# The first two experts do their down product behind their own up product, the third and later ones one expert later

## Chip, cores and metric

One core of one Trainium2 chip. The time is that of the whole kernel on the device, in microseconds; each shown time is a run of its own, and the profile is one further execution.

## What is computed

Two residual layers of a decoder for 512 tokens of width 1024. Each layer has a mixer and then a mixture of experts; the change touches the experts alone, which run once in each layer. Cut to what matters:

```python
def expert_block(args):
    xb, e = args
    return (jax.nn.silu(xb @ w1[e]) * (xb @ w3[e])) @ w2[e]
...
expert_idx = g_sel[:, None].astype(jnp.int32) * EXPERTS_PER_GROUP + top_i.astype(jnp.int32)
return routed_experts(xf, expert_idx, gates, w1, w3, w2).reshape(b, t, d)
```

There are 32 experts (numbered from 0 here), each with w1 and w3 of 1024 x 512 and w2 of 512 x 1024, in float32. Every token goes to two of them, weighted by its gates.

## The kernel before, in words

The program is written engine by engine: each engine has its own list of instructions for a stage, and semaphores join them. The router stage writes every token's normed row to `sorted_rows` in memory, behind its expert's rows. The stage `experts` then goes over the 32 experts with up to 48 rows each (`MB`):

- TensorE, `turn_rows` (L669): the expert's rows are transposed into bank `ps_x`. VectorE, `gain_rows` (L738): they are copied to `xT` with the norm's gain. There are two tiles `xT`.
- TensorE, `up_expert` (L681, L682): 8 steps with w1 and w3, 32 matmuls. ScalarE, `silu` (L799); VectorE, `hidden` (L746): the product with the second half, into `hid`. The next up product waits for it (`hid_done`, L675), as it does for `xT_out`.
- TensorE, `turn_hidden` (L703): `hid` is transposed; ScalarE, `copy_hidden` (L794), brings it to `hidT`.
- TensorE, `down_expert` (L711): 16 matmuls with w2. VectorE, `split_low` (L754, L758), and ScalarE, `split_high` (L806), cut the result into a high and a low part.
- VectorE, `select` (L771, L773): a 0/1 matrix that takes the expert's rows to tokens. TensorE, `spread` (L733): 8 matmuls with that matrix, four behind an up product and four in the middle of a down product. VectorE, `add` (L783): eight additions into `x`, weighted by the gates.

"Up n", "down n", "hidden n" and so on below are these steps for expert n.

Two orders exist. From expert `OWN` = 19 on, the down product of expert n stands behind its own up product (own order), with the spread of expert n - 1 around it. Below 19, down n stands behind up n + 1, and its spread one expert later still:

```python
for n in range(1, OWN):
    up_expert(pe, n, n - 2)
    turn_hidden(pe, n - 1)
    turn_rows(pe, slot(n + 1), use(n + 1))
    down_expert(pe, n - 1, n - 2)
```

The weights are 96 pieces of 2048 KB, numbered 3n, 3n + 1 (w1, w3 of expert n) and 3n + 2 (w2). They go round through 11 units of SBUF (`place`), so piece 11 + j may be loaded once piece j was used: once up was done for a w1 or w3, once down was done for a w2 (`freed`, L847). SyncE issues them in the order of their numbers (L583; in halves at L590 for the up weights of the last two experts), each expert's rows ahead of its pieces (L824), and waits where a piece is not free. Pieces 0 to 9 are loaded in the router stage, piece 10 at the start of `experts`; piece 11 needs up 0, 12 up 0, 13 down 0, 14 and 15 up 1, 16 down 1, 17 and 18 up 2, 19 down 2. The row load in front of pieces 12, 15 and 18 needs the turned rows of experts 1, 2 and 3.

Of the kernel before, what the change touches and what calls it, by code (L numbers as in the profile page):

```python
# [37 lines left out]
N_EXP = 32  # L38
# [582 lines left out]
def experts(nc, c, ctx, ps, x, xrows, r, gain_dram, wts, ahead):  # L621
# [33 lines left out]
    slots_made, far_out = c.sem("slots_made"), c.sem("further_slot_out")  # L655
    diag_made, row_done, row_out, own = c.sem("diag_made"), c.sem("row_done"), c.sem("row_out"), c.sem("dve_own")

    LAST, OWN = N_EXP - 1, 19
    XSLOT, XUSES = N_EXP % SLOTS, N_EXP // SLOTS
    slot = lambda n: n % SLOTS  # L660
    use = lambda n: n // SLOTS
# [3 lines left out]
    def turn_rows(pe, j, u):  # L665
        pe.wait_ge(rows_in[j], 16 * u + 16)
        nc.tensor.ldweights(c.half[:, :], tile_position=(0, 0))
        for i in range(XG):
            last = nc.tensor.transpose(ps_x[:, i:XG * P:XG], x_rows[j][:, i, :], c.ident[:, :])  # L669
        last.then_inc(xT_done, 1)  # L670
# [15 lines left out]
    def up_expert(pe, n, before):  # L686
        def first_half():
            for part in range(2):
                wts.arrived(pe, n, part)

        def second_half():
            if n in HALVED:
                for part in range(2):
                    pe.wait_ge(wts.rest_landed[HALVED.index(n)][part], 16)

        up(pe, n, n % 2, wts.view(n, 0), wts.view(n, 1), first_half, second_half)
        spread(pe, before, range(TT // 2))
# [91 lines left out]
    def gate_of(n):  # L789
        return lambda t: r.gate[:, t, n:n + 1]  # L790
# [35 lines left out]
    with nc.Block() as block:  # L826
# [56 lines left out]
        @block.tensor  # L883
        def _(pe):
            keep_warm(nc, c, ps_y[0], 40)
            for j in range(2):
                pe.wait_ge(diag_made, j + 1)
                nc.tensor.matmul(ps_c[j][:, :], c.ones[:, :], (cut, acts)[j][:, :],
                                 start=True, stop=True).then_inc(row_done, 1)
            pe.wait_ge(gain_in, 16)  # L890
            turn_rows(pe, 0, 0)
            up_expert(pe, 0, -1)
            turn_rows(pe, 1, 0)
            for n in range(1, OWN):
                up_expert(pe, n, n - 2)
                turn_hidden(pe, n - 1)
                turn_rows(pe, slot(n + 1), use(n + 1))
                down_expert(pe, n - 1, n - 2)
            turn_hidden(pe, OWN - 1)
            spread(pe, OWN - 2, range(TT // 2))  # L900
            down_expert(pe, OWN - 1, OWN - 2)
            for n in range(OWN, N_EXP):
                up_expert(pe, n, n - 1)
                if n < LAST:
                    turn_rows(pe, slot(n + 1), use(n + 1))
                turn_hidden(pe, n)
                down_expert(pe, n, n - 1)
            spread(pe, LAST, range(TT))

            def more(e, b, m):  # L910
                n, u = m + N_EXP, m + XUSES

                def landed(part):
                    pe.wait_ge(wts.landed[EXTRA[part]], 16 * m + 16 * (LOADS[EXTRA[part]] + 1))

                def extra(part):
                    return wts.unit[EXTRA[part]][:, :].rearrange("p (k n) -> p k n", k=PARTS[part])

                def first_half():
                    landed(0)  # L920
                    landed(1)

                turn_rows(pe, XSLOT, u)
                up(pe, n, 0, extra(0), extra(1), first_half, lambda: None)
                turn_hidden(pe, n)
                landed(2)
                down(pe, n, extra(2), lambda i: None)
                spread(pe, n, range(TT))

            further(pe, more)  # L930

        @block.vector
        def _(dve):
            V = nc.vector
            link = chain(dve, own)
            dve.sem_inc(low_out, 1)
            for j, tile in enumerate((cut, acts)):
                V.tensor_tensor(tile[:, :].rearrange("p (t n) -> p t n", t=TT),
                                c.ident[:, :].rearrange("p (o n) -> p o n", o=1).to_broadcast([P, TT, P]),
                                r.row[:, :, j:j + 1].to_broadcast([P, TT, P]), ALU.mult).then_inc(diag_made, 1)  # L940
            for h in range(2):
                link(V.tensor_scalar(y[:, h, :].rearrange("p (t n) -> p t n", t=TT),
                                     c.ident[:, :].rearrange("p (o n) -> p o n", o=1).to_broadcast([P, TT, P]),
                                     0.0, None, ALU.mult))
            dve.wait_ge(slots_made, 8)
            dve.wait_ge(gain_in, 16)
            gain_rows(dve, 0, 0)
            for j in range(2):
                dve.wait_ge(row_done, j + 1)
                V.tensor_copy(row_of[:, j, :], ps_c[j][:, :]).then_inc(row_out, 1)  # L950
            dve.wait_ge(row_out, 2)
            dve.sem_inc(row_out, 1)
            gain_rows(dve, 1, 1)
            hidden(dve, 0, None)
            early, late = range(TT), range(TT, GROUPS)
            for n in range(1, OWN):
                if n >= 2:
                    split_low(dve, n - 2)
                    add(dve, n - 2, early, gate_of(n - 2))
                hidden(dve, n, n)  # L960
                gain_rows(dve, n + 1, (n + 1) % 2)
                select(dve, n - 1, slot_rows(n - 1))
                if n >= 2:
                    add(dve, n - 2, late, gate_of(n - 2))
            for n in range(OWN - 2, LAST):
                if n >= 0:
                    split_low(dve, n)
                select(dve, n + 1, slot_rows(n + 1))
                if n >= OWN - 1:
                    hidden(dve, n + 1, n + 1)  # L970
                    if n + 2 <= LAST:
                        gain_rows(dve, n + 2, n % 2)
                if n >= 0:
                    add(dve, n, range(GROUPS), gate_of(n))
            split_low(dve, LAST)
            add(dve, LAST, range(GROUPS), gate_of(LAST))

            def more(e, b, m):
                n = m + N_EXP
                gain_rows(dve, n, 0)  # L980
                V.tensor_copy(far_gate[:, :], r.gate[:, :, bass.ds(e, 1)].rearrange("p t o -> p (t o)")).then_inc(far_out, 1)
                V.tensor_tensor(far[:, 0:1], r.count[:, bass.ds(e, 1)], c.block_rows[:, bass.ds(b - 1, 1)],
                                ALU.subtract).then_inc(far_out, 1)
                dve.wait_ge(far_out, 6 * m + 2)
                V.tensor_scalar(far[:, 1:2], slot0[:, :], far[:, 0:1], float(MB), ALU.add, ALU.is_ge).then_inc(far_out, 1)
                V.tensor_tensor(far[:, 2:3], slot_row[:, bass.ds(e, 1)], far[:, 0:1], ALU.add).then_inc(far_out, 1)
                dve.wait_ge(far_out, 6 * m + 4)
                V.scalar_tensor_tensor(out=far[:, 2:3], in0=far[:, 2:3], scalar=-NO_ROW, in1=far[:, 1:2],
                                       op0=ALU.add, op1=ALU.mult).then_inc(far_out, 1)
                dve.wait_ge(far_out, 6 * m + 5)  # L990
                V.tensor_scalar(far[:, 3:4], far[:, 2:3], NO_ROW, None, ALU.add).then_inc(far_out, 1)
                dve.wait_ge(far_out, 6 * m + 6)
                hidden(dve, n, None)
                select(dve, n, far[:, 3:4])
                split_low(dve, n)
                add(dve, n, range(GROUPS), lambda t: far_gate[:, t:t + 1])
                dve.wait_ge(added, GROUPS * n + GROUPS)

            further(dve, more)

        @block.scalar
        def _(act):
            act.wait_ge(row_done, 2)
            silu(act, 0)
            for n in range(1, OWN):
                if n >= 2:
                    split_high(act, n - 2)
                silu(act, n)
                copy_hidden(act, n - 1)
            copy_hidden(act, OWN - 1)  # L1010
            if OWN >= 2:
                split_high(act, OWN - 2)
            for n in range(OWN, N_EXP):
                split_high(act, n - 1)
                silu(act, n)
                copy_hidden(act, n)
            split_high(act, LAST)

            def more(e, b, m):

                n = m + N_EXP
                silu(act, n)
                copy_hidden(act, n)
                split_high(act, n)

            further(act, more)
# [1718 lines left out]
```

## Time and profile before

| | us |
|---|---|
| median of 3 runs | 1823.58 (1823.37 to 1824.29) |
| the profiled execution | 1821.84 |
| its span, first to last instruction | 1820.1 |
| TensorE matmul busy | 1656.2 (91%) |
| VectorE busy | 1167.3 (64%) |
| ScalarE busy | 489.8 (27%) |
| mean granted TensorE clock | 0.966 |

The profile gives times from the span's start. The first expert stage begins its DMA issues at 516.5 us and its last down product ends at 985 us; the second one's begin at 1326 us. "PE" is TensorE, "DVE" VectorE, "ACT" ScalarE, "SPq" SyncE's queue. A timeline row is: start, duration, engine, line and operation, output and inputs, shapes, count, and in brackets the idle time before it with what ended it. DMA instructions issued by SyncE stand at their issue, not at their landing. A granted clock of 1.00 is 2.4 GHz, 0.50 is 1.2 GHz.

### The profile page before, as it was taken

The page shows a single profiled execution, that of the slowest core. Times are in us where ns is not written, and L with a number is a line of the kernel's source. Part 1 is how long each engine was busy: PE and PEld are TensorE (multiplying, and loading weights), DVE is VectorE, ACT ScalarE, POOL GpSimd, SP SyncE. Part 2 cuts the span into 40 slices and gives each one's busy share as a digit, 9 for nine tenths or more (in the row PEclk, how much of TensorE's full clock was granted, in tenths as well). Part 3 has the DMA queues.
Part 4 walks back from the last instruction along what each step waited for, and adds up shares of the span by engine and source line. Part 5 has one row for each costly group of instructions (what it writes and reads, how often), then busy time and mean ns, then how long its engine had stood idle before and what let it go on. Part 6 is the DMA issues. An engine that isn't in the chain of part 4 may idle for free. (4 is left out here: it accounts for less than half of the span.)

```text
span 1820.1 us, 27622 instructions
## 1 busy us (share of the span) xinstructions
PE 1656.2 (91%) x10944; PEld 888.5 (49%) x11073; DVE 1167.3 (64%) x1926; ACT 489.8 (27%) x854; POOL 181.1 (10%) x234
## 2 busy tenths in 40 slices
PE   6999989989969999999997999889779999999995
PEld 4666677855533333333332779654433333333332
DVE  5467877783337677777777533693427776777766
ACT  5253334453301111111112411573211111111112
POOL 2000734411100000000000000351100000000000
PEclk9999999999979999999998999999989999999997
DMA  5541000024769999999995220206669999999993
GB/s 159 154 134 35 6 3 4 3 94 165 292 262 406 425 425 424 426 424 424 425 424 222 88 93 24 93 2 258 272 244 426 425 424 425 425 426 424 424 421 132
DMA packets 101474, 471.46 MB, mean 259 GB/s; under 512 B 29152, under 2 KB 68064, under 8 KB 75744
## 3 DMA queue, kind: packets, MB, share of 16 engines
q1 hardware_dynamic: 99040, 461.26, 63.1%
q0 software_dynamic: 2304, 8.39, 1.1%
q8 instruction: 90, 1.47, 0.3%
q14 instruction: 40, 0.33, 0.0%
HBM read 452.85 MB, written 16.78 MB: 258 GB/s over the span
## 5 line engine op out<-in xcount | busy, mean ns | idle before, releaser
L681 PE MATMUL ps<-w_unit,xT 128*48 128x512 f32 x1024 | 451.7, 594 | 6.1 <-issue 4.6
L682 PE MATMUL ps<-w_unit,xT 128*48 128x512 f32 x1024 | 451.7, 594 | 0.0
L783 DVE SCALAR_TENSOR_TENSOR x<-ps,gate_by_expert,x 128x512 f32<-128x512 f32 x512 | 348.4, 744 | 137.3 <-PE ps L733 137.2
L681 PEld LDWEIGHTS ps<-w_unit,xT 128*48 128x48 f32 x1024 | 125.9, 123 | 311.0 <-issue 309.0
L711 PE MATMUL ps<-w_unit,hidT 128*48 128x512 f32 x1024 | 248.4, 605 | 12.1 <-issue 12.1
L806 ACT ACTIVATE y_high_low<-y_cut 48x512 fp32r<-48x512 f32 x128 | 80.4, 628 | 402.2 <-DVE y_cut L754 399.7
L733 PE MATMUL ps<-y_high_low,slots_to_tokens 128*128 128x512 f32 x512 | 158.1, 430 | 14.4 <-DVE y_high_low L758 13.2
L733 PEld LDWEIGHTS ps<-y_high_low,slots_to_tokens 128*128 128x128 f32 x512 | 88.0, 192 | 131.9 <-issue 66.1
L1245 PE MATMUL ps<-hT_high,w_high 128*128 128x512 f32 (+1 forms) x344 | 139.7, 406 | 10.0 <-PE ps L1247 3.7
L1247 PE MATMUL ps<-hT_high,w_low 128*128 128x512 f32 (+1 forms) x344 | 135.9, 395 | 0.0
L1246 PE MATMUL ps<-hT_low,w_high 128*128 128x512 f32 (+1 forms) x344 | 135.5, 394 | 0.0
L682 PEld LDWEIGHTS ps<-w_unit,xT 128*48 128x48 f32 x1024 | 125.9, 123 | 0.0
L711 PEld LDWEIGHTS ps<-w_unit,hidT 128*48 128x48 f32 x1024 | 60.3, 123 | 120.8 <-issue 120.8
L746 DVE TENSOR_TENSOR gate_act_hid<-gate_act_hid,ps 48x512 f32<-48x512 f32 x64 | 44.3, 692 | 111.0 <-ACT gate_act_hid L799 92.4
L353 PE MATMUL ps<-w_unit,yT 128*128 128x512 f32 x256 | 113.7, 596 | 1.7 <-PEq L78 1.7
L799 ACT ACTIVATE gate_act_hid<-ps 48x512 f32<-48x512 f32 x64 | 37.9, 592 | 274.1 <-PE ps L682 274.1
L754 DVE TENSOR_SCALAR y_cut<-ps 48x512 int32<-48x512 int32 x128 | 87.5, 684 | 5.5 <-PE ps L711 3.6
L758 DVE TENSOR_TENSOR y_high_low<-ps,y_cut 48x512 fp32r<-48x512 f32 x128 | 88.2, 689 | 4.0
L1443 POOL TENSOR_SCALAR_AFFINE_SELECT keep<-keep 128x256 f32<-128x256 f32 x32 | 20.4, 638 | 666.3 <-ACT keep L1420 666.2
L1245 PEld LDWEIGHTS ps<-hT_high,w_high 128*128 128x128 f32 (+1 forms) x344 | 64.3, 187 | 42.5 <-issue 27.1
L353 PEld LDWEIGHTS ps<-w_unit,yT 128*128 128x128 f32 x256 | 47.3, 190 | 54.6 <-issue 54.6
L1247 PEld LDWEIGHTS ps<-hT_high,w_low 128*128 128x128 f32 (+1 forms) x344 | 64.2, 187 | 15.9
(368 smaller groups left out, 2232.6 us busy)
## 6 DMA issues: line engine op xcount, KB each, us to landing
w_unit<-in_moe_w SPq DMA_DIRECT2D x184, 2048.0 KB, 27.4
w_unit<-in_moe_w SPq DMA_DIRECT2D x16, 1024.0 KB, 33.4
x_rows<-sorted_rows SPq DMA_DIRECT2D x64, 192.0 KB, 26.9
w_unit<-in_od_w_qkv SPq DMA_DIRECT2D x12, 1024.0 KB, 5.3
w_raw<-in_ev_w_in SPq DMA_DIRECT2D x10, 1024.0 KB, 6.9
sorted_rows<-bias SPq DMA_DIRECT2D x32, 192.0 KB, 5.6
w_unit<-in_ev_w_out SPq DMA_DIRECT2D x2, 2048.0 KB, 11.6
w_unit<-in_od_w_out SPq DMA_DIRECT2D x2, 2048.0 KB, 11.6
```

The source lines that it names most:

```text
L353: last = nc.tensor.matmul(ps_out[2 * (i % 2) + h][:, :], yT[:, f, tok(i)], w[h][:, f, :], start=f == 0, stop=f == KD - 1)
L681: nc.tensor.matmul(ps_1[0:MB, :], xT[b][:, k, :], w1[:, k, :], start=k == 0, stop=k == KD - 1)
L682: last = nc.tensor.matmul(ps_3[UP:UP + MB, :], xT[b][:, k, :], w3[:, k, :], start=k == 0, stop=k == KD - 1)
L711: last = nc.tensor.matmul(ps_y[h][half[h], :], hidT[:, k, :], w2[:, k, h * FF:(h + 1) * FF], start=k == 0, stop=k == KF - 1)
L733: nc.tensor.matmul(ps_c[t % 2 * 2 + h][:, :], sel_of(n)[:, t * P:(t + 1) * P], y[:, h, :], start=True, stop=True).then_inc(spread_out, 1)
L754: nc.vector.tensor_scalar(cut[half[h], :].bitcast(I32), ps_y[h][half[h], :].bitcast(I32), HIGH_BITS, None, ALU.bitwise_and).then_inc(maske ...
L758: nc.vector.tensor_tensor(y[half[1 - h], h, :], ps_y[h][half[h], :], cut[half[h], :], ALU.subtract).then_inc(low_out, 1)
L783: nc.vector.scalar_tensor_tensor(out=xs, in0=ps_c[i % 4][:, :], scalar=gate(t), in1=xs, op0=ALU.mult, op1=ALU.add).then_inc(added, 1)
L806: nc.scalar.activation(y[half[h], h, :], cut[half[h], :], ACT.Copy).then_inc(high_out, 1)
L1245: nc.tensor.matmul(out, lhsT[0], rhs[0], start=start, stop=False)
L1246: nc.tensor.matmul(out, lhsT[0], rhs[1], start=False, stop=False)
L1247: return nc.tensor.matmul(out, lhsT[1], rhs[0], start=False, stop=stop)
```

## The change

A number `EARLY` = 2 is added. Experts 0 and 1 go in own order, expert 2's up stands by itself, and from expert 3 to 18 the order is the old one. VectorE's and ScalarE's lists follow.

```diff
-    LAST, OWN = N_EXP - 1, 19
+    LAST, OWN, EARLY = N_EXP - 1, 19, 2
...
             turn_rows(pe, 0, 0)
-            up_expert(pe, 0, -1)
-            turn_rows(pe, 1, 0)
-            for n in range(1, OWN):
+            for n in range(EARLY):
+                up_expert(pe, n, n - 1)
+                turn_rows(pe, slot(n + 1), use(n + 1))
+                turn_hidden(pe, n)
+                down_expert(pe, n, n - 1)
+            up_expert(pe, EARLY, -1)
+            turn_rows(pe, slot(EARLY + 1), use(EARLY + 1))
+            for n in range(EARLY + 1, OWN):
                 up_expert(pe, n, n - 2)
                 turn_hidden(pe, n - 1)
                 turn_rows(pe, slot(n + 1), use(n + 1))
...
             hidden(dve, 0, None)
+            select(dve, 0, slot_rows(0))
+            for n in range(EARLY - 1):
+                split_low(dve, n)
+                select(dve, n + 1, slot_rows(n + 1))
+                hidden(dve, n + 1, n + 1)
+                gain_rows(dve, n + 2, n % 2)
+                add(dve, n, range(GROUPS), gate_of(n))
+            hidden(dve, EARLY, EARLY)
+            gain_rows(dve, EARLY + 1, (EARLY + 1) % 2)
             early, late = range(TT), range(TT, GROUPS)
-            for n in range(1, OWN):
-                if n >= 2:
-                    split_low(dve, n - 2)
-                    add(dve, n - 2, early, gate_of(n - 2))
+            for n in range(EARLY + 1, OWN):
+                split_low(dve, n - 2)
+                add(dve, n - 2, early, gate_of(n - 2))
                 hidden(dve, n, n)
                 gain_rows(dve, n + 1, (n + 1) % 2)
                 select(dve, n - 1, slot_rows(n - 1))
-                if n >= 2:
-                    add(dve, n - 2, late, gate_of(n - 2))
+                add(dve, n - 2, late, gate_of(n - 2))
...
             silu(act, 0)
-            for n in range(1, OWN):
-                if n >= 2:
-                    split_high(act, n - 2)
+            copy_hidden(act, 0)
+            for n in range(1, EARLY):
+                split_high(act, n - 1)
+                silu(act, n)
+                copy_hidden(act, n)
+            silu(act, EARLY)
+            for n in range(EARLY + 1, OWN):
+                split_high(act, n - 2)
                 silu(act, n)
                 copy_hidden(act, n - 1)
```

TensorE, first stage, behind up 0 (+ is the change, - is before; `x_rows_332` are expert 1's rows, units 273 and 274 its w1 and w3, unit 272 is expert 0's w2):

```order
 L667 LDWEIGHTS half
 L669 MATMUL ps<-ident,x_rows_332 128x128 x3
+L701 LDWEIGHTS half
+L703 MATMUL ps<-ident,gate_act_hid 128x48 x4
+L711 MATMUL ps<-w_unit_272,hidT 48x512 x8
 L681 MATMUL ps<-w_unit_273,xT_335 48x512
 L682 MATMUL ps<-w_unit_274,xT_335 48x512
```

Turn hidden 0 and down 0 moved ahead of up 1.

TensorE, the same stage, behind up 2 (units 276 and 277 are expert 2's w1 and w3, 224 and 330 expert 3's, 275 is expert 1's w2):

```order
 L682 MATMUL ps<-w_unit_277,xT_334 48x512
-L733 MATMUL ps<-y_high_low,slots_to_tokens_343 128x512 x4
-L701 LDWEIGHTS half
-L703 MATMUL ps<-ident,gate_act_hid 128x48 x4
 L667 LDWEIGHTS half
 L669 MATMUL ps<-ident,x_rows_331 128x128 x3
-L711 MATMUL ps<-w_unit_275,hidT 48x512 x4
-L733 MATMUL ps<-y_high_low,slots_to_tokens_343 128x512 x4
-L711 MATMUL ps<-w_unit_275,hidT 48x512 x4
 L681 MATMUL ps<-w_unit_224,xT_335 48x512
 L682 MATMUL ps<-w_unit_330,xT_335 48x512
```

Between up 2 and up 3 only expert 3's rows are turned now; expert 0's spread and down 1 went ahead of up 2.

VectorE in the same stage, from the split of expert 0's result to the split of expert 1's, before:

```order
L754 TENSOR_SCALAR y_cut<-ps 48x512 x2
L758 TENSOR_TENSOR y_high_low<-ps,y_cut 48x512 x2
L783 SCALAR_TENSOR_TENSOR x<-ps,gate_by_expert,x 128x512 x4
L746 TENSOR_TENSOR gate_act_hid<-gate_act_hid,ps 48x512
L738 TENSOR_TENSOR xT_335<-ps,gain 128x384
L771 TENSOR_SCALAR first_choice<-row_of_token,slot_row 128x512
L773 SCALAR_TENSOR_TENSOR slots_to_tokens_344<-row_of_token,slot_row,first_choice 128x512
L783 SCALAR_TENSOR_TENSOR x<-ps,gate_by_expert,x 128x512 x4
L754 TENSOR_SCALAR y_cut<-ps 48x512 x2
```

and in the change:

```order
L754 TENSOR_SCALAR y_cut<-ps 48x512 x2
L758 TENSOR_TENSOR y_high_low<-ps,y_cut 48x512 x2
L771 TENSOR_SCALAR first_choice<-row_of_token,slot_row 128x512
L773 SCALAR_TENSOR_TENSOR slots_to_tokens_344<-row_of_token,slot_row,first_choice 128x512
L746 TENSOR_TENSOR gate_act_hid<-gate_act_hid,ps 48x512
L738 TENSOR_TENSOR xT_334<-ps,gain 128x384
L783 SCALAR_TENSOR_TENSOR x<-ps,gate_by_expert,x 128x512 x8
L746 TENSOR_TENSOR gate_act_hid<-gate_act_hid,ps 48x512
L738 TENSOR_TENSOR xT_335<-ps,gain 128x384
L754 TENSOR_SCALAR y_cut<-ps 48x512 x2
```

Select 1 and hidden 1 stand ahead of expert 0's additions, which are no longer in two parts, and hidden 2 with the gain of expert 3's rows stands ahead of the split of expert 1's result.

## Rows read from the trace of the kernel before

**Rows 1.** Windows: us, busy by engine (x instructions), PEclk, DMA share, GB/s
```profile
core 0: us, PE busy (x) PEld busy (x) DVE busy (x) ACT busy (x) POOL busy (x), PEclk, DMA share, GB/s
606.00:706.00 100.00, 100.00 (x453) 38.02 (x465) 72.27 (x113) 15.25 (x28) 0.00 (x0) 1.00 1.01 425
850.00:945.00 95.00, 91.94 (x416) 34.87 (x426) 69.54 (x109) 14.33 (x26) 0.00 (x0) 1.00 1.01 424
```

**Rows 2.** Waits of TensorE's matmuls, 535 to 786 us: total, times, longest
```profile
PE ps L681 <- issue: 2.3, 1, 2.3
```

**Rows 3.** Timeline, one expert in own order, TensorE and VectorE, 802 to 818 us
```profile
802.82 1.19 PE L733 MATMUL ps<-y_high_low,slots_to_tokens 128*128 128x512 f32 x4
...
804.49 0.68 PE L703 MATMUL ps<-ident,gate_act_hid 48*128 48x48 f32 x4
805.63 1.92 PE L711 MATMUL ps<-w_unit,hidT 128*48 128x512 f32 x8 [0.47 <-issue]
...
810.37 0.59 PE L681 MATMUL ps<-w_unit,xT 128*48 128x512 f32 x1
...
817.34 1.20 PE L733 MATMUL ps<-y_high_low,slots_to_tokens 128*128 128x512 f32 x4
...
803.63 0.69 DVE L746 TENSOR_TENSOR gate_act_hid<-gate_act_hid,ps 48x512 f32<-48x512 f32 x1 [3.47 <-ACT gate_act_hid L799]
```

**Rows 4.** Timeline of TensorE, experts 0 to 4 of the first stage
```profile
531.74 0.55 PE L669 MATMUL ps<-ident,x_rows 128*128 128x128 f32 x3
534.57 0.60 PE L681 MATMUL ps<-w_unit,xT 128*48 128x512 f32 x1 [2.29 <-issue]
...
542.83 3.64 PE L711 MATMUL ps<-w_unit,hidT 128*48 128x512 f32 x16
546.28 0.59 PE L681 MATMUL ps<-w_unit,xT 128*48 128x512 f32 x1
...
560.29 0.59 PE L681 MATMUL ps<-w_unit,xT 128*48 128x512 f32 x1
...
574.28 0.59 PE L681 MATMUL ps<-w_unit,xT 128*48 128x512 f32 x1
```

**Rows 5.** Issue and landing of expert 31's last up halves, and its up's start
```profile
L590 SPq DMA_DIRECT2D w_unit<-in_moe_w x2: 1106/1642/2177, 942.3 to 943.4; - x2
...
DMA to landing us min/median/max: 26.2/26.9/27.6
...
970.37 0.59 PE L681 MATMUL ps<-w_unit,xT 128*48 128x512 f32 x1
```

**Rows 6.** Timeline of VectorE, hidden 0, hidden 1 and the gain behind it
```profile
533.78 0.69 DVE L746 TENSOR_TENSOR gate_act_hid<-gate_act_hid,ps 48x512 f32<-48x512 f32 x1 [0.90 <-ACT gate_act_hid L799]
542.40 0.69 DVE L746 TENSOR_TENSOR gate_act_hid<-gate_act_hid,ps 48x512 f32<-48x512 f32 x1 [7.93 <-PE ps L703]
543.12 0.56 DVE L738 TENSOR_TENSOR xT<-ps,gain 128x384 f32<-128x384 f32 x1
```

**Rows 7.** Timeline of SyncE's queue: issues of pieces 11 to 13 and of 16
```profile
531.80 0.33 SPq L583 DMA_DIRECT2D w_unit<-in_moe_w  x1
...
532.68 0.43 SPq L583 DMA_DIRECT2D w_unit<-in_moe_w  x1
...
546.50 0.80 SPq L583 DMA_DIRECT2D w_unit<-in_moe_w  x2
...
560.50 0.80 SPq L583 DMA_DIRECT2D w_unit<-in_moe_w  x2
```

**Rows 8.** Windows of the first stage's start, last column GB/s
```profile
532.00:546.00 14.00, 11.67 (x58) 4.71 (x60) 3.51 (x6) 2.66 (x4) 0.00 (x0) 1.00 0.79 315
546.50:578.00 31.50, 31.50 (x144) 11.99 (x146) 23.06 (x36) 5.62 (x10) 0.00 (x0) 1.00 0.98 404
```

**Rows 9.** DMA issues: count, KB each, median us to landing
```profile
w_unit<-in_moe_w SPq DMA_DIRECT2D x184, 2048.0 KB, 27.4
...
x_rows<-sorted_rows SPq DMA_DIRECT2D x64, 192.0 KB, 26.9
```

**Rows 10.** Second stage: a window in expert 1, and the first row behind a stop
```profile
1344.00:1349.00 5.00, 5.00 (x16) 1.62 (x16) 0.00 (x0) 0.00 (x0) 0.00 (x0) 0.66 1.00 420
...
1599.43 2.04 PE L733 MATMUL ps<-y_high_low,slots_to_tokens 128*128 128x512 f32 x4 [3.36 <-DVE y_high_low L758]
```

## The prediction

> **What bounds the kernel now.** I read the windows by stretch first, then TensorE's waits, the timeline where the orders differ, SyncE's queue, and last the late landings. In an expert stage both candidates look full: in 100 us of the first stage's middle TensorE is busy 100.00 us and the DMA moves 425 GB/s at a share of 1.01; near the stage's end (850 to 945) it is 91.94 of 95 us and 424 GB/s [rows 1]. A full queue is not a bound. What counts is whether TensorE ever stands still for weights, and between 535 and 786 us the table of waits has one entry for a matmul, 2.3 us at the first expert's hand-over, where it waits for VectorE [rows 2]. Later, with own order (below), the 3 us missing are about six gaps of 0.47 us in front of a down product [rows 3], again no weights. So the end of a stage is set by TensorE's own list of work: 13.99 us an expert with the down one expert later (560.29 to 574.28) [rows 4], 14.52 us in own order (6.97 us from an up to the spread behind it, 810.37 to 817.34, and 7.55 us from that spread to the next up, 802.82 to 810.37) [rows 3].
>
> The weights keep a reserve to the end. The last halves of expert 31's up weights are issued at 942.3 to 943.4 and land 26.2 to 27.6 us later, by 971.0 us at the latest; its up begins at 970.37 us and wants that second half half an up later, about 973.9 us [rows 5]. That is about 3 us of reserve after 30 experts: small, but enough for no gap.
>
> **The change, part by part.** No matmul, vector or DMA instruction is added or dropped; only orders move, the same in both expert stages. I follow the first from 534.57 us, where up 1 starts before the change. Up 4 starts at 574.28 us [rows 4], so before takes 39.71 us for up 1, 2, 3, down 0, 1, 2 and the spreads of experts 0 and 1. The same work stands between these two places after the change.
>
> 1. Hidden 0 and down 0 now stand before up 1. Hidden 0 ends at 533.78 + 0.69 = 534.47 us [rows 6], the same as before. In own order the transposes of the hidden start 0.17 us behind the product (803.63 + 0.69 = 804.32, then 804.49) and the down 1.14 us behind those, 0.47 us of it an idle gap for ScalarE's copy [rows 3]; together 1.31 us, so down 0 starts at 535.78. A down without a spread hands over after 3.45 us (542.83 to 546.28) [rows 4]: up 1 starts at 539.23, 4.66 us later than before.
> 2. Expert 1 then runs as an expert of the later stretch does: 14.52 us [rows 3]. Its add, select and split stand in the order that VectorE has there, so this is a measured whole. Up 2 starts at 553.75.
> 3. The crossing back. Behind up 2 there is neither a spread nor a down, only the turning of expert 3's rows, and up 3 waits for two VectorE steps in a row: the product of hidden 2, then the gain on the turned rows. The product starts 0.81 us behind the place where the spread would start (803.63 against 802.82) [rows 3], so at 553.75 + 6.97 + 0.81 = 561.53, and takes 0.69; the gain starts 0.03 behind it (542.40 + 0.69, then 543.12) and takes 0.56 [rows 6]: 562.81. Up 1 started 0.10 us behind its release (534.57 against 534.47) [rows 4, 6]: up 3 starts at 562.9, 9.15 us behind up 2. About 1.6 us of that is idle, a **new wait**; bounds are 0 (an expert whose up follows a down, as at 560.29) and the 2.29 us of the first hand-over [rows 4], which holds a table load that is not repeated here. I take 1.6 because its parts have rows.
> 4. Up 3 to up 4 is the old pattern, 13.99 us: up 4 starts at 576.9.
>
> The sum is 4.66 + 14.52 + 9.15 + 13.99 = 42.3 us against 39.7: **+2.6 us a stage**, made of the two 0.47 us copy gaps, the 1.6 us wait and hand-overs of some 0.05 us. Nothing later gives it back, since TensorE has no slack behind. Bounds a stage are +1.0 (the new wait at 0) and +3.3 (at 2.29).
>
> What the DMA gains. SyncE may load piece 13 only once down 0 is done: it is issued at 546.50, after 532.68 had been the last, and the following burst at 560.50 [rows 7]. From 532 to 546 us the DMA moves only 315 GB/s on average [rows 8], which is the 4.4 MB of two pieces and one row load; at full rate they are through by about 543.7, and the DMA is then empty. With down 0 done at about 539.4 this hole closes. But the next one opens. From the issue at 531.80 on stand eight pieces of 2048 KB and three row loads of 192 KB [rows 7, 9] before piece 19, that is 17.4 MB or 40.9 us at 425 GB/s; with the 1.6 us that a start from empty loses (over the 31.5 us behind 546.5 the mean is 404 GB/s where a full stretch has 425: 31.5 x 21 / 425) [rows 1, 8] they are through at 574.2. Piece 19 needs down 2, which before was done 0.2 us behind up 4's start and now is at 577.1; with a start from empty its data count from 578.7. Before, piece 19 follows without a hole: 546.50 + 1.6 + 13.0 MB / 425 = 578.7. So the weight stream after the change is where it was, within a microsecond: the hole of some 4.5 us has only moved from 544 to 574. The reserve of 3 us at the stage's end grows by what TensorE loses, and buys nothing in this change.
>
> All else costs nothing: the selects moved on VectorE run while TensorE is in its 7 us up products, where VectorE is idle (7.9 us in front of 542.40) [rows 6]; were that cover gone, a select is about 1 us. ScalarE waits most of each expert.
>
> Two stages: +5.2 us. The profiled execution took 1821.84 us (span 1820.1), so its sum is 1827.0; the median of the runs, 1823.58, lies 1.74 higher, and gives **1828.8 us**, +0.28%. A measurement of this kernel tells about 0.2%, 3.6 us, from no change.
>
> **The rivals.**
>
> *The clock adds to it.* Behind a stop of 3.36 us TensorE runs on at half clock (1.2 GHz) in the second stage, 1599.43 us; and in that stage's expert 1, behind the 2.29 us stop, the granted clock averages 0.66 over 5 us, 5 x 0.34 = 1.7 us lost [rows 10]. The first stage has the same stop and no such stretch. The new 1.6 us wait is one more occasion in each stage, and the first stop, now followed by a second short one, may catch it too: one or two extra stretches, 1830.5 to 1832.2 us. For it: two of the three stops named lose the clock. Against: the new one is the shortest. [...]
>
> *The clock gives back.* That one stretch of the second stage need not come again where the order behind the stop is another. Then 1.7 us fall off: 5.2 - 1.7 = 3.5 us, 1827.1 us, which counts as no change. Nothing in the rows decides it. A shorter new wait gives the same result from the other side.
>
> *The weights decide, and it is faster.* If somewhere an up or down waits for a landing, closing the hole at 544 pulls each such wait forward by up to 4.4 us a stage, provided the second hole stays closed (down 2 done before 574.2): 1823.6 - 8.8 = 1814.8 us. It decides only from the point where the reserve at the end is gone; the rows show 3 us of it and no gap. The Trainium skill (Perfetto Trace Analysis, Identifying the Most-Contended Engine) says to improve the most contended engine; with the DMA at its full rate that is the DMA here, and by that rule this rival is what one gets. The table of waits speaks against it.
>
> **How the numbers follow.** Forecast, TensorE's list 2.6 us longer in each stage, with the clock as it was: 0.63. Clock adds: 0.14. Clock gives back, or the wait is near its lower bound (+1.0 a stage is 1825.6): 0.18. Weights decide: 0.05. Faster 0.05, same 0.18, slower 0.77. The range runs from the lower bound of the new wait, 1825.6, to two extra half-clock stretches, 1832.2; it leaves out the fast case and the far ends of the clock cases.
>
> **What would show it.** Right: in the first stage up 1 starts near 539.2, up 2 near 553.7, up 3 near 562.9 behind an idle 1.6 us, up 4 near 576.9, and every later row of TensorE stands 2.6 us later with no new gap; SyncE issues at 539.5, 546.4, 554, 561 and 577.1; the DMA is empty for some 3 us before 577 and not at 545. Wrong: up 4 starts by 575.5 us; or gaps before an up vanish later in the stage, which would mean that weights were awaited after all; or the stage's last down ends less than 1.5 us later than at present.

## The result, and the profile after

The change made the kernel slightly slower. Five runs of it gave a median of 1831.03 us against 1823.58 us for five of before, 7.45 us more. The ratio on record is 1.0049 (95% interval 1.0035 to 1.0062), which is 8.9 us; it is not the quotient of the two medians, which would be 1.0041. A second set, 12 runs against 35 of before on one chip, gave 1829.0 against 1822.88 us and a ratio of 1.0034 (1.0022 to 1.0047), 6.1 us. Forecast were 5.2 us and at most 8.6: the first set's ratio lies just beyond that and its median inside, the second set lies inside by both.

| us | before | after |
|---|---|---|
| median, first set | 1823.58 | 1831.03 |
| median, second set | 1822.88 | 1829.0 |
| profiled execution | 1821.84 | 1828.59 |
| its span | 1820.1 | 1826.8 |
| TensorE matmul busy | 1656.2 | 1656.8 |
| mean granted clock | 0.966 | 0.965 |

The two profiled executions differ by 6.75 us, so their traces must account for that. TensorE's timeline after, first stage, beside [rows 4] (start, duration, engine, line, output and inputs; idle before in brackets):

```profile
531.91 0.55 PE L669 MATMUL ps<-ident,x_rows 128*128 128x128 f32 x3
534.81 0.68 PE L703 MATMUL ps<-ident,gate_act_hid 48*128 48x48 f32 x4 [2.35 <-DVE gate_act_hid L746]
535.95 5.34 PE L711 MATMUL ps<-w_unit,hidT 128*48 128x512 f32 x16 [0.47 <-issue]
541.09 0.59 PE L681 MATMUL ps<-w_unit,xT 128*48 128x512 f32 x1
...
550.88 1.92 PE L711 MATMUL ps<-w_unit,hidT 128*48 128x512 f32 x8 [0.47 <-issue]
...
555.62 0.59 PE L681 MATMUL ps<-w_unit,xT 128*48 128x512 f32 x1
...
562.62 0.55 PE L669 MATMUL ps<-ident,x_rows 128*128 128x128 f32 x3
564.73 0.63 PE L681 MATMUL ps<-w_unit,xT 128*48 128x512 f32 x1 [1.55 <-DVE xT L738]
...
578.75 0.59 PE L681 MATMUL ps<-w_unit,xT 128*48 128x512 f32 x1
```

Read it down the list. Down 0 starts behind a 2.35 us stop and a 0.47 us copy gap. (The stop holds ScalarE's table load, 1.28 us at 531.86 in the kernel before; there is none at the later wait for up 3.) Expert 1 takes 14.53 us (541.09 to 555.62). The new wait is there, 1.55 us ahead of up 3, released by VectorE's gain on the turned rows (`xT`, L738); up 2 to up 3 is 9.11 us and up 3 to up 4 14.02. Each was forecast to within 0.05 us. One row was not: down 0 takes 5.34 us where it took 3.64 [rows 4]. From the turned rows of expert 1 to up 4 it was 42.54 us before (531.74 to 574.28), and is 46.84 now: 4.30 us more, 2.6 of it the list and 1.7 that row. Its cause is in the clock. Windows of the changed kernel, the last three columns the granted clock, the DMA share and GB/s:

```profile
536.00:541.00 5.00, 5.00 (x16) 1.70 (x18) 0.00 (x0) 0.00 (x0) 0.00 (x0) 0.66 1.03 436
541.00:576.00 35.00, 32.95 (x152) 12.36 (x154) 18.05 (x28) 4.94 (x9) 0.00 (x0) 1.00 0.99 403
577.00:580.00 3.00, 3.00 (x15) 0.94 (x16) 3.00 (x6) 0.00 (x0) 0.00 (x0) 1.00 0.12 33
```

At a mean of 0.66 over 5 us TensorE loses 1.7 us. In the second stage such a stretch hits down 0 too (0.66 from 1348 to 1353), where before it hit up 1 [rows 10]; so there the change costs its list alone, 46.79 us between the same two places (1344.74 to 1391.53) for 44.24 (1341.04 to 1385.28). Together 4.30 + 2.55 = 6.85 us against the 6.75 measured.

The remaining places moved by some tenths and nearly cancel. From up 4 to up 31 the first stage is 0.4 us shorter than before and the second 0.2 us longer, most of it between up 18 and up 20 (40.18 us before and 39.93 after, 41.01 and 41.37). There the stop of 3.36 us stands, and the half-clock stretch behind it differs from run to run. The first stage of the kernel before has it too, beside the second stage's in [rows 10]:

```profile
788.43 1.75 PE L733 MATMUL ps<-y_high_low,slots_to_tokens 128*128 128x512 f32 x4 [3.36 <-DVE y_high_low L758]
790.10 2.94 PE L711 MATMUL ps<-w_unit,hidT 128*48 128x512 f32 x8
```

The third line of the windows is the DMA's new hole: share 0.12 between 577 and 580, where before it was 1.01. The hole at 544 is gone (share 0.98 from 543 to 546, where it was 0.19 from 543 to 547). SyncE's queue, beside [rows 7]:

```profile
541.32 0.33 SPq L583 DMA_DIRECT2D w_unit<-in_moe_w  x1
548.19 0.33 SPq L583 DMA_DIRECT2D w_unit<-in_moe_w  x1
...
555.83 0.33 SPq L583 DMA_DIRECT2D w_unit<-in_moe_w  x1
562.70 0.33 SPq L583 DMA_DIRECT2D w_unit<-in_moe_w  x1
...
578.96 0.81 SPq L583 DMA_DIRECT2D w_unit<-in_moe_w  x2
```

These are pieces 13, 14, 16, 17 and 19. Piece 13 is asked for 5 us earlier than before (546.50), piece 19 waits for down 2. At the stage's end the weights come 1.7 us later than in [rows 5], the last up halves issued at 944.0 to 945.1 with the same 26.2 to 27.6 us to landing, and up 31 starts at 974.42, 4.05 us later:

```profile
L590 SPq DMA_DIRECT2D w_unit<-in_moe_w x2: 1106/1642/2177, 944.0 to 945.1; - x2
...
DMA to landing us min/median/max: 26.2/26.9/27.6
...
974.42 0.59 PE L681 MATMUL ps<-w_unit,xT 128*48 128x512 f32 x1
```

So the reserve of the weights at the stage's end grew by about 2.4 us (4.05 less 1.7), and TensorE did not need it.

The end is not where the reserve is smallest. Take it as the time from the landing of an expert's w3 to the start of its up. Issue and landing of expert 18's w3 and the start of up 18, before and then after:

```profile
L583 SPq DMA_DIRECT2D w_unit<-in_moe_w x1: 328/328/328, 742.4 to 742.4; - x1
DMA to landing us min/median/max: 27.3/27.3/27.3
770.19 0.59 PE L681 MATMUL ps<-w_unit,xT 128*48 128x512 f32 x1
...
L583 SPq DMA_DIRECT2D w_unit<-in_moe_w x1: 328/328/328, 746.8 to 746.8; - x1
DMA to landing us min/median/max: 24.7/24.7/24.7
774.56 0.59 PE L681 MATMUL ps<-w_unit,xT 128*48 128x512 f32 x1
```

Before, the reserve is 19.9 us at up 4, falls by 1.2 to 2.1 us an expert and is only 0.5 us at up 18 (0.8 in the second stage). Up 19, behind the crossing to own order, has 9.9 us again. The change has 3.1 and 2.8 us at up 18.

### The profile page after: what moved, and what is told of

The parts are those of the page before. It is cut to its first block and busy times, and to the rows that moved or that the text cites. A ratio compares the mean times of both kernels' runs of the same rounds, so it can differ in the third digit from the quotient of the medians.

```text
span 1826.8 us, 27622 instructions
## 1 busy us (share of the span) xinstructions
PE 1656.8 (91%) x10944; PEld 889.4 (49%) x11073; DVE 1167.3 (64%) x1926; ACT 489.5 (27%) x854; POOL 180.8 (10%) x234
```

## The experiments

Ratios are to the kernel before on the same chip, with 95% intervals. There are three sets of runs, on three chips, each with the kernel before beside it: medians of 1822.88, 1822.67 and 1823.47 us. The first holds the change once more, only expert 0 and the first two with filled stops; the second piece 13, the crossings at 27 and at 23; the third the rest. Single runs of any kernel here spread over some 5 to 12 us (before: 1817.5 to 1828.4), so the medians of 12 carry about 2 us and the places in the traces carry the argument. Where part of that spread comes from can be seen: up 0 of the first stage starts between 521.1 and 527.6 us in the profiles of kernels that are alike up to there, so it arises ahead of the experts.

**The change once more**, as a second sample.

> The changed kernel once more, nothing altered. List theory (TensorE's list is 2.6 us longer in each expert stage, and every stop of TensorE above 1.5 us may be followed by a half-clock stretch that costs 1.7 us): the runs lie between 1828.6 and 1834.1 us in steps of about 1.7, and the profile of this run shows, against the first profile of the change, its extra time as half-clock stretches behind a stop and nowhere as a gap in front of an up or down product. Weights theory (the second hole in the DMA makes an up wait in the slower runs): an idle gap of 1 us or more in front of some up product late in a stage, with the clock full.

Measured: 1829.0 us (1826.57 to 1833.17), ratio 1.0034 (1.0022 to 1.0047). Its profile, at 1827.84 us, has up 1, 2, 3 and 4 of the first stage at 539.68, 554.19, 563.30 and 577.33, the same distances, down 0 stretched in both stages (6.49 and 5.34 us), and no gap ahead of an up product late in a stage. The places of the list theory hold. Its picture of the runs does not: five of the 12 lie below 1828.6 us, they spread without steps of 1.7 us, and behind the 1.55 us stop there is no stretch.

**Only expert 0 in own order.**

```diff
-    LAST, OWN, EARLY = N_EXP - 1, 19, 2
+    LAST, OWN, EARLY = N_EXP - 1, 19, 1
```

> Only expert 0 goes in own order (EARLY = 1), the crossing back stands behind up 1. List theory: one copy gap of 0.47 us and one crossing stop of 1.6 us a stage remain, so 2.1 us a stage instead of 2.6, and half-clock stretches as in the change: 1827.8 us with the clock as in before's runs, 1829 to 1831 with a stretch more in each stage; at most 1 to 2 us below the change. Weights theory: the early request of the weights is as early as in the change (down 0 is at the same place), so all of the change's loss that comes from the later hole (down 2) goes: within 1 us of before, 1823 to 1825.

Measured: 1826.72 us, ratio 1.0017 (1.0004 to 1.0029). That is 2.3 us below the change, 3.8 above before by medians and 3.1 by the ratio, between what the two theories expected, so that the median does not decide. The trace decides: from up 0 to up 4 53.36 us (527.54 to 580.90) against 49.59 before, 3.77 more, of which 1.68 is down 0 at half clock (5.32 us for 3.64) and 2.09 the list, as expected 2.1; no up product waits for weights. The crossing stop is the same as the change's:

```profile
552.88 0.63 PE L681 MATMUL ps<-w_unit,xT 128*48 128x512 f32 x1 [1.55 <-DVE xT L738]
```

**The change, its stops filled.** TensorE multiplies zeros in bf16 in each stop, into banks free at that time.

```diff
                 turn_rows(pe, slot(n + 1), use(n + 1))
+                if n == 0:
+                    keep_warm(nc, c, ps_y[0], 36)
                 turn_hidden(pe, n)
+                pe.wait_ge(low_out, 2 * n + 1)
+                keep_warm(nc, c, ps_y[0], 6)
                 down_expert(pe, n, n - 1)
             up_expert(pe, EARLY, -1)
             turn_rows(pe, slot(EARLY + 1), use(EARLY + 1))
+            pe.wait_ge(added, 5)
+            keep_warm(nc, c, ps_c[0], 24)
```

> The change, with small bf16 matmuls of zeros in TensorE's new and old stops of the stage's start (36 before the transposes of hidden 0, 6 in each copy gap, 24 behind up 2), so that TensorE is busy there and waits no longer than before. List theory: up 1 to up 4 start at the same distances as in the change, less the half-clock stretches; 2 x 2.6 = 5.2 us above before at most, less what before itself loses to such stretches in the same place (up to 3.4): 1825 to 1829 us, with a spread of the runs under 2 us, and 2 to 6 us below the change. If the clock has no part in it: equal to the change, 1831. Weights theory: equal to the change.

Measured: 1824.78 us, ratio 1.0005 (0.9991 to 1.0018), 4.2 us below the change. Its stop and down 0:

```profile
532.55 2.17 PE L107 MATMUL ps<-half 128*128 128x128 bf16 x36
535.06 0.68 PE L703 MATMUL ps<-ident,gate_act_hid 48*128 48x48 f32 x4 [0.34 <-DVE gate_act_hid L746]
535.67 0.51 PE L107 MATMUL ps<-half 128*128 128x128 bf16 x6
536.21 3.64 PE L711 MATMUL ps<-w_unit,hidT 128*48 128x512 f32 x16
```

The first row is the filler, and down 0 is back at 3.64 us. From 536 to 541 us the granted clock is 1.00 at a DMA share of 1.00, where the change had 0.66 at 1.03. The stretch is thus a matter of the clock behind a stop and not of contention with the DMA. One part was missed: the runs were to spread by less than 2 us and spread by 7.3, so the stretches are not what spreads them.

**The kernel before, its stop filled.**

```diff
             turn_rows(pe, 1, 0)
+            keep_warm(nc, c, ps_y[0], 36)
             for n in range(1, OWN):
```

> The kernel before, with 36 small bf16 matmuls of zeros in its one stop of 2.3 us (ahead of up 1). List theory: it loses up to 1.7 us a stage there to a half-clock stretch in some of its runs, the profiled one in the second stage only: 1820 to 1823.4 us, that is 0 to 3.4 us faster than before. If no stretch is caused by this stop: 1823.6, or up to 0.3 slower where the filler holds up 1 back. Weights theory says nothing else here.

Measured: 1819.08 us, ratio 0.9979 (0.9966 to 0.9992), 3.8 us faster than before, 0.4 us more than the most that was expected. So before loses to this stop too. From up 0 to up 4 of the first stage it takes 49.59 us, the filled change 52.21 (525.12 to 577.33): 2.62 us of pure list, and two stages of it are 5.2 us, beside a difference of 5.7 us between the two medians. That pair prices the change without this clock loss. It also shows that filling gained nearly as much in before (3.8 us) as in the change (4.2 us): between medians the clock's share in the change's loss is 0.4 us, too small to tell from nothing, while the two executions that were profiled first differ by a whole stretch.

**Piece 13 held back.** The change's order, but the DMA's early hole is opened again.

```diff
                 sp.wait_ge(down_done if was == 2 else up_done, gone + 1)
+                if (n, part) == (4, 1):
+                    sp.wait_ge(up_done, 2)
```

> The change, but SyncE holds piece 13 (w3 of expert 4) back until up 1 is done, though its unit is free since down 0. That opens the DMA's hole at 544 us again. List theory: the weights are not awaited and the later hole behind piece 18 absorbs it, so the time is that of the change, within 1.5 us (1827.5 to 1830.5 beside 1829.0), TensorE's starts unchanged. Weights theory: what the change gains by the earlier request is lost: 3 to 8 us slower than the change.

Measured: 1830.78 us, 0.3 us above the expected band, ratio 1.0040 (1.0025 to 1.0055), beside 1.0034 for the change: within the intervals the same. From up 0 to up 4 the two stages take 53.74 and 53.90 us, beside 53.88 and 53.83 in the change. The windows show the hole back at 544 and the later one gone (up 4 starts at 576.19 here):

```profile
541.00:547.00 6.00, 6.00 (x29) 2.29 (x26) 2.39 (x4) 0.59 (x1) 0.00 (x0) 1.00 0.21 57
547.00:576.00 29.00, 26.94 (x124) 10.09 (x128) 16.03 (x26) 3.10 (x6) 0.00 (x0) 1.00 0.99 416
577.00:580.00 3.00, 3.00 (x16) 0.91 (x14) 2.91 (x5) 1.25 (x2) 0.00 (x0) 1.00 0.95 328
```

What the change wins for the DMA early it gives back at piece 19, and holding the piece costs nothing that can be measured.

**The crossing to own order at expert 27, without and with the change.** This asks when the weights do matter. In both kernels only `OWN = 19` becomes `OWN = 27`.

> The kernel before, with the crossing to own order at expert 27 instead of 19: eight experts more save 0.53 us each, 4.2 us a stage. List theory with a reserve of 3 us in the weights: TensorE runs into the weights, so that gaps appear ahead of late up products and only about 3 us a stage are gained: 1816 to 1818.5 us, with gaps of 1 us or more in front of up 30 or up 31. If the reserve is larger than reckoned: 8.4 us faster than before, 1814.5, no gap.

Measured: 1833.16 us, ratio 1.0058 (1.0040 to 1.0077): 10 us slower, where 4 to 8 us faster were expected. The expectation took the reserve at the stage's end for the reserve everywhere. In the order with the down one expert later TensorE needs 13.99 us an expert and the DMA about 15.2; the reserve of 19.9 us at up 4 is used up behind up 18, and up 19 waits. The waits of TensorE's matmuls, 780 to 910 us, and the row ahead of up 20:

```profile
PE ps L681 <- DMA w_unit<-in_moe_w: 9.6, 8, 2.0
```

```profile
804.02 0.60 PE L681 MATMUL ps<-w_unit,xT 128*48 128x512 f32 x1 [1.02 <-DMA w_unit<-in_moe_w]
```

Up 19 to up 26 all wait, 1.0 us and more each. The starts are then 15.2 us apart (804.02, 819.26, 834.48), the pace of the weights, but for one 16.2 us step ahead of up 24. Up 31 starts 6.5 us behind the landing of its last weights (973.7, then 980.18): the reserve that the crossing gives back comes too late to be used.

> The change with the same crossing at 27. Its TensorE list is 2.6 us longer and its half-clock stretches add up to 1.7 us a stage, at a weight stream that ends at most 1.7 us later, so its reserve is larger. List theory: the full 8.4 us are gained against the change, 1820.6 us, no gap ahead of an up product; what it stands above before_own27 is 2 to 6 us. If the order of the first two experts is what lets the later crossing pay (the weights decide as soon as TensorE's list is shorter): equal to or faster than before_own27.

Measured: 1835.68 us, ratio 1.0068 (1.0051 to 1.0085), 2.5 us above the kernel without the change. Missed in the same way; but the pair tells the reserve apart. Here the first waits of the first stage are those of up 20, 0.35 us, and of up 21:

```profile
818.27 0.60 PE L681 MATMUL ps<-w_unit,xT 128*48 128x512 f32 x1 [1.06 <-DMA w_unit<-in_moe_w]
```

The change moves the first wait from up 19 to up 20 or 21, and not because the weights are clearly earlier: counted from up 0 of its own stage, up 21, which waits for its weights in both, starts at 293.3 us without the change (525.93 to 819.26) and at 294.9 with it (523.42 to 818.27), and in the second stage at 293.7 (1342.98 to 1636.66) and 292.9 (1344.75 to 1637.66). The two kernels with filled stops, which have no stretch at the start, show it best: in the first stage expert 18's w3 lands 244.9 us behind up 0 without the change and 245.0 with it, and up 18 starts 245.5 and 248.1 us behind it. TensorE arrives later, at weights that come when they did. The difference of 2.5 us between the two medians lies in the expected 2 to 6.

**The change with the crossing at 21**, which spends that reserve.

> The change with own order from expert 21 instead of 19. With the crossing at 27, the first up product with a gap was up 19 without the change and up 20 with it (0.36 us; full gaps from up 21), so the change buys one to two experts of the faster order. List theory with that reserve: 2 x 2 x 0.53 = 2.1 us less than the change, less a gap of 0.4 us in front of up 20 in each stage: 1827.2 us beside 1829.0, still above before. If the weights bind earlier than that: equal to the change or slower, with gaps ahead of up 19 and up 20.

Measured: 1826.34 us, ratio 1.0023 (1.0009 to 1.0037), still slower than before. It is below the change by 2.7 us between medians of two sets and by 2.0 us between the ratios; those intervals overlap, so that a gain over the change is likely and not shown. The weights are awaited in one up product of the two stages, for 0.4 us. The order of the first two experts costs 2.6 us a stage and lets two experts more save 0.53 us each in the own order.

**Two versions meant to beat both.** The first is the kernel before with fillers in the first stop and in the 3.36 us stop at the crossing, and the crossing at 23; of its edit the filler at the crossing is shown:

```diff
...
+            pe.wait_ge(added, GROUPS * (OWN - 3) + 5)
+            keep_warm(nc, c, ps_c[0], 56)
             spread(pe, OWN - 2, range(TT // 2))
```

> A version that should beat both: the kernel before with filler matmuls in the stage's first stop (36) and in the 3.36 us stop where own order begins (56), and that crossing at 23. List theory: 3.8 us for the first filler as measured, about 1.6 to 2.4 us a stage for the half-clock stretch behind the second stop, 2.1 us a stage for four experts fewer in own order: 1822.9 - 3.8 - 4 - 4.2 = 1811 us, 1809 to 1815; above that by what the weights' reserve of 3 us falls short.

Measured: 1822.93 us, ratio 1.0006 (0.9994 to 1.0018). It waits for weights in three up products of one stage and four of the other (3.6 and 4.7 us), and one of those stops has a half-clock stretch behind it. Missed by 12 us, of which these waits and the stretch are 10, for the reason found with the crossing at 27. With the crossing left at 19:

> The kernel before with filler matmuls in its first stop (36) and in the 3.36 us stop at the crossing (56), the crossing left at 19. List theory: 3.8 us as with the first filler alone, and 1.6 to 2.4 us a stage for the half-clock stretch behind the second stop: 1814.5 to 1816 us, that is 0.995 to 0.9965 of before, with no gap ahead of an up product. If the weights take the gain back: gaps ahead of up 19 or later and 1818 to 1819 us, as with the first filler alone.

Measured: 1817.25 us, ratio 0.9967 (0.9951 to 0.9983), 6.2 us faster by medians, no wait for weights. The stop at the crossing:

```profile
785.83 3.30 PE L107 MATMUL ps<-half 128*128 128x128 bf16 x56
789.25 1.16 PE L733 MATMUL ps<-y_high_low,slots_to_tokens 128*128 128x512 f32 x4
790.34 1.93 PE L711 MATMUL ps<-w_unit,hidT 128*48 128x512 f32 x8
```

Those rows are at full clock, where before the same two took 1.75 and 2.94 us (788.43 and 790.10 above), and in the second stage the spread took 2.04 [rows 10]. The median stands 1.3 us above the expected band, while its interval reaches into it.

The second version is the change with fillers in its stops at the stage's start and at the crossing, and the crossing at 21.

> The change at its best: fillers in all its stops, the one of the crossing too, and own order from expert 21. List theory: 5.2 us for the change's longer list, minus 2.1 us for two experts, on top of warm_own19: 3.1 us above it, 1817.5 to 1819.5 us. If the early request of the weights pays once TensorE is kept at full clock: equal to warm_own19 or faster.

Measured: 1818.43 us, ratio 0.9978 (0.9963 to 0.9993). It is 1.2 us above the version without the change, where 3.1 were expected; the two intervals overlap, so that the order of the two is not shown. It is inside its expected range.

## Why the prediction was right or wrong

- *TensorE's list sets the end of a stage.* Right. Neither trace has a wait for weights. In the first stage of the two kernels with filled stops the 2.62 us of the start are 2.7 us at its end (up 0 to up 31: 448.31 for 445.61). In the second they are 4.0 us (449.27 for 445.30), of which 1.4 are a longer stretch at the crossing.
- *Steps 1 to 4, +2.6 us a stage.* Right in every part: 0.47 and 0.47 us for the copies, 1.55 us for the new wait where 1.6 stood; in the two kernels with filled stops the sum is 2.62 us.
- *The DMA's hole moves from 544 to 574.* Right in kind: it stands between 576 and 580, 2 us later than said, as down 2 comes later by the stretch in down 0. Holding piece 13 back cost nothing measurable.
- *"With the clock as it was", given 0.63.* **This is the step that failed.** The forecast kept one half-clock stretch in two stages, that is 0 us for the clock, and made a further one a rival at 0.14. With down 0 behind the stop, the stretch came in all 12 stage starts that were profiled (six kernels with the new order and no filler), lengthening down 0 by 1.3 us at least, 2.9 at most and mostly 1.7. Up 1 behind the same stop had it in three of four. The term that was mis-sized is therefore the clock's: 0 in the forecast, +1.7 us between the profiled executions, and 5.2 + 1.7 = 6.9 us is close to their difference of 6.75. How much of it is in the medians stays open: filling the stops took off 4.2 us in the change and 3.8 in before. The "one stretch" was itself partly luck, as the kernel before with the crossing at 27, alike in its first 19 experts, had it in both stages.
- *The rival on the clock.* Half right. The first stop did catch the stretch in the stage where before had none; the new 1.55 us wait never did, the up product behind it took 7.07 to 7.08 us in all 12 stage starts. Its count of "two of the three stops" left out the 3.36 us stop of the first stage, which also lost the clock. The Trainium skill (TensorE: Matmul & The Clock Gate, HAM oscillation) tells of a kernel in which waits for the DMA between short pieces of matmul work let the clock fall anew each time. Those waits are longer than the stop of 2.3 us here; the traces show it for this shorter stop too, and for no stop of 1.55 us.
- *The range.* Its upper end stood 8.6 us above before. The first set gave 1.0049, which is 8.9 us; the second, larger one 1.0034, 6.2 us, inside. One stretch more, 6.9 us, does not reach 8.9 either. The other 2 us stay open; five runs of a kernel whose runs spread over some 10 us can give them, and the three runs of before had let that spread appear as 1 us.
- *The reserve of about 3 us "after 30 experts".* Right for the end and wrong as a picture of the stage. The reserve is smallest at up 18, 0.5 us, where the old order has nearly run it down. This did not touch the forecast, as the weights come when they did and TensorE later.
- *The rival on the weights, given 0.05.* It did not happen: closing the early hole pulled no wait forward, since none was there. The Trainium skill (Perfetto Trace Analysis, Identifying the Most-Contended Engine) says to optimize the most contended engine first. In this change that gained nothing, but with the crossing at 27 the DMA does decide how far the faster order may go: the table of waits is empty because the crossing stands just ahead of the point where it would fill.

## What to carry to other kernels

An empty table of waits shows that a queue is not awaited now, not how near it is: put a number on the reserve at each place where the order changes, and move that place once to see where waits begin. An order that asks for data earlier was worth nothing here, because a later piece of the same queue was asked for later, so follow the queue until it is full for good. And price a stop of TensorE with what runs behind it: here 2.3 us of waiting mostly cost another 1.7 in the work that followed, and filling that stop with 36 matmuls of zeros in both stages gave 3.8 us (1.5 to 6.2 by the interval of the ratio).

## What was not expected of the hardware

- A stop of 2.3 us on TensorE was followed by a half-clock stretch of 1.7 us cost in 15 of 16 profiled stage starts without a filler, and in none of 10 with one. A stop of 1.55 us had none in 12.
- The stretch need not begin at the stop: in the second stage before, two pairs of up 1 still ran at full clock after the 2.29 us stop, and only then did the granted clock go to 0.50.
- A DMA stream of about 425 GB/s gave an up product every 15.2 us when TensorE waited for it, with six of the eight waits showing as a steady gap of 1.0 us and not as one long one.
- The runs spread over 7.3 us with the stops at the stage's start filled too, so that most of the spread of single runs has another cause, which stays open.
